# A fused decoder layer: one hidden combination split before it is stored, and an order of work moved

## What is computed

```
x = x + gate2 * (square(relu(h @ w_mlp1)) @ w_mlp2)      # w_mlp1 1024 x 4096, w_mlp2 4096 x 1024
```

## Time and profile before

| what | us |
|---|---|
| median of 3 runs (lowest, highest) | 1138.2 (1137.73, 1141.65) |
| the profiled execution's own time | 1139.7 |
| its span, first to last instruction | 1137.8 |
| PE busy | 1092.3 (96%) |
| DVE busy | 769.6 (68%) |
| ACT busy | 441.9 (39%) |
| POOL busy | 248.7 (22%) |
| TensorE's granted clock, mean share of 2.4 GHz | 0.988 |

### The profile page before, as it was taken

How to read it: one execution, slowest core, us unless ns; L and a number is a source line. 1 busy time by engine, 2 the same in 40 slices (tenths; PEclk the granted TensorE clock), 3 DMA queues, 4 the chain that set the end, 5 groups by cost and what they waited for, 6 DMA issues and landing times. The chain is left out here.

```text
span 1137.8 us, 14053 instructions
## 1 busy us (share of the span) xinstructions
PE 1092.3 (96%) x5210; PEld 882.9 (78%) x5210; DVE 769.6 (68%) x1206; ACT 441.9 (39%) x746; POOL 248.7 (22%) x219
## 2 busy tenths in 40 slices
PE   5999999999999999998999999999899899999998
PEld 4678877777778988776788888887678788787787
DVE  5673556565446767799676767677886957848752
ACT  6342334354444335662333323233522514416231
POOL 2011000000001105213222222223223314232231
PEclk9999999999999999998999999999999999999999
DMA  9967333332013013104535353537626345335205
GB/s 272 275 185 259 128 114 111 112 111 74 28 38 122 29 47 93 38 0 144 180 114 191 113 193 112 194 111 251 229 93 226 145 148 187 100 121 222 74 1 148
DMA packets 150932, 151.71 MB, mean 133 GB/s; under 512 B 14116, under 2 KB 124880, under 8 KB 147280
## 3 DMA queue, kind: packets, MB, share of 16 engines
q1 hardware_dynamic: 142800, 122.45, 33.5%
q0 software_dynamic: 8064, 28.36, 7.6%
HBM read 113.04 MB, written 37.75 MB: 133 GB/s over the span
## 5 line engine op out<-in xcount | busy, mean ns | idle before, releaser
L745 PE MATMUL ps<-cmb_hi,wm_hi 128*128 128x512 f32 x880 | 349.2, 397 | 25.7 <-DVE x1t L2162 9.9
L746 PE MATMUL ps<-cmb_lo,wm_hi 128*128 128x512 f32 x880 | 345.3, 392 | 0.0
L747 PE MATMUL ps<-cmb_hi,wm_lo 128*128 128x512 f32 x880 | 345.1, 392 | 0.0
L745 PEld LDWEIGHTS ps<-cmb_hi,wm_hi 128*128 128x128 f32 x880 | 166.8, 190 | 69.4 <-DVE x1t L2162 12.7
L747 PEld LDWEIGHTS ps<-cmb_hi,wm_lo 128*128 128x128 f32 x880 | 166.8, 190 | 35.3
L746 PEld LDWEIGHTS ps<-cmb_lo,wm_hi 128*128 128x128 f32 x880 | 166.9, 190 | 34.5 <-issue 0.5
L745 PE MATMUL ps<-act_hi,w_hi 128*128 128x512 f32 x400 | 162.2, 405 | 3.0 <-DVE act_lo L1688 3.0
L746 PE MATMUL ps<-act_lo,w_hi 128*128 128x512 f32 x400 | 156.7, 392 | 0.0
L747 PE MATMUL ps<-act_hi,w_lo 128*128 128x512 f32 x400 | 156.7, 392 | 0.0
L1398 ACT ACTIVATE wm_hi<-wm_f 128x512 fp32r<-128x512 f32 x128 | 77.3, 627 | 197.7 <-POOL wm_f L715 151.8
L2162 DVE SCALAR_TENSOR_TENSOR x1t<-ps,ada,x1t 128x512 f32<-128x512 f32 x112 | 83.5, 746 | 81.5 <-PE ps L747 81.5
(11 more groups left out here) (200 smaller groups left out, 1413.8 us busy)
## 6 DMA issues: line engine op xcount, KB each, us to landing
raw<-in_w_mlp_dram SPq DMA_DIRECT2D x128, 256.0 KB, 3.9
cmb_f<-h_spill SPq DMA_DIRECT2D x22, 1024.0 KB, 4.9
wada<-in_w_ada_dram POOLq DMA_DIRECT2D x32, 512.0 KB, 5.0
h_spill<-stage SPq DMA_DIRECT2D x16, 768.0 KB, 6.3
w_raw<-in_w_in_dram SPq DMA_DIRECT2D x18, 512.0 KB, 3.8
ada_rows<-in_w_ada_dram SPq DMA_DIRECT2D x16, 512.0 KB, 7.4
h_spill<-stage SPq DMA_DIRECT2D x32, 256.0 KB, 3.3
h_spill<-stage SPq DMA_DIRECT2D x16, 512.0 KB, 6.7
```

The source lines that it names most:

```text
L745: pe.matmul(bank, wh, hi, start=first, stop=False, skip_group_check=onto)
L746: pe.matmul(bank, wh, lo, start=False, stop=False, skip_group_check=onto)
L747: return pe.matmul(bank, wl, hi, start=False, stop=last, skip_group_check=onto)
```

## The change

T2 is no longer stored whole and split again for each chunk. In the up phase ScalarE rounds T2's slot of stage into a new tile sums_high (`hidden_hi`), VectorE subtracts it in place (`hidden_lo`), and SyncE stores the two as two transfers of 256 KB into a new tensor split_spill (`store_split`); T1 and T3 are stored as 512 KB. For a chunk, T2 is loaded as two transfers of 1 MB straight into cmb_hi and cmb_lo, and product S2 of a chunk's first step waits for both landings (32) in place of low pieces. combination_hi and both_lo of T2 are gone. sums_high takes 2 KB of x1t's last tile, so that tile is stored at the start of the up phase and loaded back at step 18 (512 KB each), and add_product(19, 3) waits for it.

The order is changed: at pair 2 e1(3) and c11(3) come later, SyncE's order at pairs 2, 14 and 15 is another (T1, T3 and T2 of chunk 0 are loaded before pair 14's stores), e2(15) moves from pair 15 to step 16, T1's low pieces stand after S1's weights, T3's first low piece ahead of add_product(w, 0), and step 16's list of VectorE is rearranged; chunk 1's early loads go from step 17 to step 18. Left out of the diff: new semaphores, the size of h_spill (6 in place of 7 combinations) and split_spill, and the renumbering of `piece`.

```diff
--- before
+++ after
@@ -90,9 +90,14 @@
...
     _more = _p + 1 < PAIRS
+    if _p == 2:
+        UP_COPIES += [("e5", 2), ("e1", 3), ("e2", 2)]
+        UP_SUMS += [("e25", 2), ("c22", 2), ("c11", 3), ("c12", 2), ("c21", 2)]
+        SQUARES += [("b21", 1), ("b11", 2), ("b22", 2), ("b11", 3), ("b12", 2)]
+        continue
     UP_COPIES += [("e1", _p + 1)] * _more + [("e5", _p), ("e2", _p)]
     UP_SUMS += [("c11", _p + 1)] * _more + [("e25", _p), ("c22", _p), ("c12", _p), ("c21", _p)]
-    SQUARES += [("b21", _p - 1)] + [("b11", 2)] * (_p == 2) + [("b11", _p + 1)] * _more + [("b22", _p), ("b12", _p)]
+    SQUARES += [("b21", _p - 1)] + [("b11", _p + 1)] * _more + [("b22", _p), ("b12", _p)]
 SQUARES += [("b21", PAIRS - 1)]
@@ -104,8 +109,9 @@
-FIRST_LOADS = (B11, B21, T1, T2, T3, B22, NT4)
-STORED = (B11, B22, T1, T2, T3, B21, NT4)
+STORED = (B11, B22, T1, T3, B21, NT4)
+STORED_SPLIT = (T2,)
+PIECES = (B11, B21, T1, T3, B22, NT4)
@@ -166,6 +172,7 @@
...
         stage = at("stage", [8, HALF], TMPB)
+        sums_high = at("sums_high", [len(STORED_SPLIT), HALF], REG + 28 * KB, F32R)
         early = [at(f"early{i}", [HK, HALF], TMPB + 8 * i * KB) for i in range(2)]
@@ -562,11 +572,20 @@
...
                 sp.wait_ge(s_tt, 4 * p + 3)
-                store(p, s_stt, slice(2, 5), slice(ST_T1, ST_T3 + 1))
+                store(p, s_stt, slice(2, 4), slice(ST_T1, ST_T3 + 1, 2))
...
                 sp.wait_ge(s_tt, 4 * p + 4)
-                store(p, s_stb21, slice(5, 7), slice(ST_B21, ST_NT4 + 1))
+                store(p, s_stb21, slice(len(STORED) - 2, len(STORED)), slice(ST_B21, ST_NT4 + 1))
+            def store_split(p):
+                q, j = divmod(p, CHUNK_PAIRS)
+                sp.wait_ge(s_hth, p + 1)
+                sp.dma_start(split_spill[q, 0, :, :, j, :].rearrange("i p n -> p i n"),
+                             sums_high[:, :, :].bitcast(F32)).then_inc(s_sth, 16)
+                sp.wait_ge(s_htl, p + 1)
+                sp.dma_start(split_spill[q, 1, :, :, j, :].rearrange("i p n -> p i n"),
+                             stage[:, SPLIT_SLOTS, :]).then_inc(s_stl, 16)
@@ -574,17 +593,29 @@
...
                 sp.wait_ge(s_pd, PRODUCT[PAIRS - 1 + CHUNK_PAIRS * q, i])
-                load_combination(q, i, cmb_f[i])
+                if i in STORED_SPLIT:
+                    n = STORED_SPLIT.index(i)
+                    sp.dma_start(cmb_hi[i][:, :, :].bitcast(F32), split_spill[q, 0, n]).then_inc(s_cl[i], 16)
+                    sp.dma_start(cmb_lo[i][:, :, :].bitcast(F32), split_spill[q, 1, n]).then_inc(s_cl[i], 16)
+                else:
+                    load_combination(q, i, cmb_f[i])
             def hidden_stored(q):
-                for s in (s_stb11, s_stb22, s_stt, s_stb21):
+                for s in (s_stb11, s_stb22, s_stt, s_stb21, s_sth, s_stl):
                     sp.wait_ge(s, 16 * CHUNK_PAIRS * (q + 1))
+            sp.wait_ge(s_evb, 2 * N_OUT)
+            sp.dma_start(x_spill[KT - 1], x1t[:, KT - 1, :]).then_inc(s_x1out, 16)
             for p in range(PAIRS):
+                if p == PAIRS - 1:
+                    load_in_place(0, T1)
                 sp.wait_ge(s_wlm, SPLIT[p, A22])
...
                 load_pair(p + 2)
+                if p == PAIRS - 1:
+                    load_in_place(0, T3)
+                    load_in_place(0, T2)
                 if p:
@@ -593,23 +624,33 @@
...
                 if p == 1:
+                    store_split(0)
                     store_b22(1)
...
                     store_b11(2)
+                    store_b22(2)
+                    store_b11(3)
+                    store_split(1)
+                    continue
+                if p + 1 == PAIRS:
+                    store_split(p - 1)
                 if p + 1 < PAIRS:
                     store_b11(p + 1)
+                    store_split(p - 1)
                     if p == PAIRS - 2:
...
                     store_b22(p)
-            for i in FIRST_LOADS[2:]:
+            for i in (B22, NT4):
                 load_in_place(0, i)
...
                 q, pp = divmod(w - PAIRS, CHUNK_PAIRS)
+                if w == PAIRS + 2:
+                    store_split(PAIRS - 1)
                 if w + 2 < 2 * PAIRS:
@@ -617,12 +658,14 @@
...
                     store_b21(PAIRS - 1)
-                if pp == 1 and q + 1 < CHUNKS:
+                if pp == (1 if q else 2) and q + 1 < CHUNKS:
                     hidden_stored(q + 1 if q else CHUNKS - 1)
...
                     load_combination(q + 1, B21, early[1])
+                if w == PAIRS + 2:
+                    sp.dma_start(x1t[:, KT - 1, :], x_spill[KT - 1]).then_inc(s_x1in, 16)
                 if pp == CHUNK_PAIRS - 1 and q + 1 < CHUNKS:
@@ -1149,7 +1192,10 @@
...
                 def wait_part(j):
-                    if j % 2 == 0:
+                    if i in STORED_SPLIT:
+                        if j == 0:
+                            pe.wait_ge(s_cl[i], 32 * (q + 1))
+                    elif j % 2 == 0:
                         pe.wait_ge(s_clo, piece(q, i, j // 2))
@@ -1478,6 +1524,15 @@
...
+            def hidden_hi(p):
+                act.wait_ge(s_tt, 4 * p + 3)
+                if p == 0:
+                    act.wait_ge(s_h2, 2 * KT)
+                    act.wait_ge(s_x1out, 16)
+                wait(act, s_sth, 16 * p)
+                act.activation(sums_high[:, :, :], stage[:, SPLIT_SLOTS, :], ACT.Copy).then_inc(s_hth, 1)
             def combination_hi(q, i):
@@ -1511,24 +1566,28 @@
...
                         e1(2)
-                    if p + 1 < PAIRS:
+                    elif p + 1 < PAIRS:
                         e1(p + 1)
...
                     e5(p)
+                    if p + 1 < PAIRS:
+                        hidden_hi(p - 1)
                 if p and p + 1 < PAIRS:
...
                 weight_hi(p + 1, S1)
+                if p == 2:
+                    e1(3)
                 if p == 0:
                     weight_hi(1, A22)
+                elif p + 1 < PAIRS:
+                    e2(p)
                 else:
-                    e2(p)
+                    hidden_hi(p - 1)
                 if p == PAIRS - 1:
...
                 weight_hi(p + 1, S2)
-                if p == PAIRS - 1:
-                    combination_hi(0, T2)
                 weight_hi(p + 1, S4)
@@ -1552,6 +1611,8 @@
...
                     combination_hi(q, B22)
+                if w == PAIRS:
+                    e2(PAIRS - 1)
                 if ends:
@@ -1564,14 +1625,13 @@
...
                     weight_hi(w + 1, S3)
-                if ends:
-                    combination_hi(q + 1, T2)
-                if more:
                     weight_hi(w + 1, S1)
...
                     weight_hi(w + 1, S2)
+                if w == PAIRS + 1:
+                    hidden_hi(PAIRS - 1)
                 if ends:
@@ -2020,6 +2080,7 @@
...
                 dve.wait_ge(s_sq, n_b12(p))
+                wait(dve, s_stl, 16 * p)
                 dve.tensor_tensor(stage[:, ST_T1, :], b12, b11, ALU.subtract).then_inc(s_tt, 1)
@@ -2030,6 +2091,12 @@
...
                 dve.tensor_tensor(stage[:, ST_NT4, :], stage[:, ST_B21, :], stage[:, ST_T2, :], ALU.subtract).then_inc(s_tt, 1)
+            def hidden_lo(p):
+                dve.wait_ge(s_hth, p + 1)
+                dve.wait_ge(s_tt, 4 * p + 4)
+                dve.tensor_tensor(stage[:, SPLIT_SLOTS, :].bitcast(F32R), stage[:, SPLIT_SLOTS, :], sums_high[:, :, :].bitcast(F32),
+                                  ALU.subtract).then_inc(s_htl, 1)
@@ -2095,6 +2162,7 @@
...
             weight_lo(3, A12)
+            hidden_lo(0)
             squared(ST_B22, n_c22(1))
@@ -2110,14 +2178,13 @@
...
                 last_sum(p - 1)
-                if p == 2:
-                    c11(2)
-                    squared(0, n_c11(2))
                 if p + 1 < PAIRS:
-                    c11(p + 1)
-                    squared((p + 1) % 2, n_c11(p + 1))
+                    b = p + (p > 2)
+                    c11(b)
+                    squared(b % 2, n_c11(b))
                     weight_lo(p + 2, A11)
                     weight_lo(p + 2, A12)
+                    hidden_lo(p - 1)
                 else:
@@ -2125,13 +2192,18 @@
...
                     weight_lo(p + 1, S3)
+                    if p == 2:
+                        c11(3)
+                        squared(1, n_c11(3))
                     c12(p)
...
                     both_lo(0, B21)
-                    both_lo(0, T1)
                     weight_lo(p + 1, S3)
                 weight_lo(p + 1, S1)
+                if p + 1 == PAIRS:
+                    hidden_lo(p - 1)
+                    both_lo(0, T1)
                 weight_lo(p + 1, S2)
@@ -2151,12 +2223,16 @@
...
                 yield
+                hidden_lo(p)
+                yield
...
                 m, e = 2 * ((w - PAIRS) % CHUNK_PAIRS) + o, 7 * (w - PAIRS) + i
+                if (w, i) == (PAIRS + CHUNK_PAIRS - 1, 3):
+                    dve.wait_ge(s_x1in, 16)
```

(34 more changed lines are left out.)

12 lines of the change are left out of this document (8 added, 4 removed).

## The result

| kernel | median, us (lowest, highest) | profiled execution: time, span |
|---|---|---|
| before | 1138.76 (1137.73, 1141.65), 6 runs | 1139.7, 1137.8 |
| after | 1130.99 (1129.01, 1133.45), 6 runs | 1129.01, 1127.2 |

The ratio is 0.9928, 95% interval 0.9916 to 0.9939: 0.7% faster, 7.8 us. The forecast was 14.9 us less, 1123.3, in a range that ended at 1130.0. The direction was right, the size about half, and the result lies outside the range.

A forecast was written before the change was run, and what follows sets the result against it. TensorE, busy 96% of the span, was taken as the bound, with only idle time and clock to win. Terms -3.1 - 4.4 + 0.6 - 8.0 = -14.9 took 1138.2 to 1123.3 us, range 1118.5 to 1130.

The forecast's parts named there:

- Pair 2: Up phase, pair 2: the pauses before products S4 and A22 both go, -3.1 us.
- Pairs 3 to 14: Up phase, forecast for pairs 3 to 13: the split's added copy and subtraction stay hidden, cost 0.
- Steps 17 to 19: Step 17: hidden_lo(15) ahead of add_product(18, 0) lengthens the wait of product S2, 0.76 already, by +0.6 us.
- Borders: Three later chunk borders: one pause of about 1.3 us stays at each, the second goes, -8.0 us together.
- The handover: Pair 15 and step 16, up to down: 10.8 us lost becomes 6.4, -4.4 us.
- The pause of 3.46 goes: Step 16, before product T2: T1 lands earlier, VectorE runs through, and the 3.46 us wait disappears.
- T2's low part is the fifth megabyte from then: Handover load queue: counted from T1's issue at about 786.8 us, T2's low part lands near 803.
- 1.7 for a clock that does not fall: Handover: a stretch of half clock after a pause goes, 1.7 us of the -4.4.
- Its pause grows from 2.20 to 2.7: Pair 15, product A22: B21 lands 0.5 us later, so the wait for c22 grows to 2.7 us.
- NT4's forecast pause of 1.5: Step 16: NT4's pieces and weight A11 ahead of add_product(16, 4) make product NT4 wait 1.5 us.
- the handover gives nothing: Rival: B21 lands 3 to 4 us late, product A22's pause grows as much, +4.4, 1127.7 us; chance 0.11.
- The rival that both falls stay: Rival: the clock falls as often as before, both dips stay, +3.4, 1126.7 us; chance 0.17.

The follow-up runs named there:

- x4: Kernel before with only pair 2's new order (e1(3), c11(3) later, stores reordered), T2 stored whole: 1134.71 us, ratio 0.9966.
- x3: Kernel after with T2's low part loaded behind T1 at the three chunk borders: 1130.23 us, ratio 0.9934.
- the repeats: Kernel after, unchanged, run twice more: 1133.81 us (ratio 0.9947) and 1131.51 us (0.9923).
- x2: Kernel after with chunk 0's loads of B22 and NT4 issued ahead of pair 14's stores: 1133.37 us, ratio 0.9951.
- x6: Kernel after with pair 15's A22 weights rounded on ScalarE ahead of the copies of B11 and B21: 1128.97 us, ratio 0.9908.
- y1: Kernel after with the store of x1t's last tile, and its wait, behind pair 2's raw weight loads: 1130.61 us, ratio 0.9923.
- y2: Kernel after with the moves of x3, x5, x6 and y1, hidden_lo(1) behind pair 2's square, sums between B11's and NT4's low pieces: 1120.06 us, ratio 0.9829.
- x1: Kernel after with B22's first low piece in step 16 moved behind add_product(16, 2): 1132.96 us, ratio 0.9950.
- x5: Kernel after with x2's early loads, e2(15) behind NT4's high copy and A11's weights behind NT4's sum: 1127.61 us, ratio 0.9896.

## Why the prediction came out as it did

**Pair 2: right mechanism, one length off.** x4's stage is 3.1 shorter, as forecast. The forecast counted the new subtraction as one of five slots "of about 0.65 us"; it measured 1.79 beside GpSimd in the profiled run, and product A22 waited 0.62 for c22. That the Trainium skill has VectorE and GpSimd shut each other out (SBUF — State Buffer, Who interferes with whom) was cited for NT4's pieces and not applied here; the row agrees with it.

**Pairs 3 to 14: right**, no pause in any execution.

**Steps 17 to 19: right**, 1.36 against 0.76.

**Borders: right.** T1 was late for the reason given, which x3 shows for about half of the pause; the pause that stayed was 1.26 where 1.3 stood, NT4's went: -7.6 against -8.0. The forecast's own sum had a slip: a pause of 1.3 with its 0.29 is 1.6 and not 1.4, which makes the three borders -7.4.

**The handover: the failed step.** "The pause of 3.46 goes": it did. The step that failed is the load queue, the sentences "T2's low part is the fifth megabyte from then: 4.8 + 4 x 2.4 + some 2 for the raw weights among them, near 803" and, built on it, "B22 and NT4 ... land near 810 and 812", with T3's pause put at 0.65. The forecast has T2's low part 16.4 us behind T1's issue and B22 23.2 us behind it (786.8 to 810). In the kernel after, T1 left at 783.15, T2's low part landed 18.9 us later (issued at 789.35, 12.7 us to landing) and B22 25.9 us later. The last 7 us, from T2's low part to B22, are as forecast; the stretch up to it was priced 2.5 us too short, although the forecast counted it high: T1, the raw weights, T3 and T2's two parts are five megabytes with the raw weights in, which at 4.8 + 4 x 2.4 would be 14.4. T3 waited 3.15 for it. That stretch, with the columns of the earlier trace rows:

```profile
783.00:786.00 3.00, 3.00 (x15) 2.49 (x14) 0.58 (x1) 2.38 (x3) 1.38 (x2) 1.00 0.56 182
786.00:807.00 21.00, 17.54 (x77) 13.84 (x76) 20.08 (x23) 8.37 (x12) 4.70 (x3) 1.00 0.98 355
```

For the first 3 us the queue held T1 alone, since the raw weights behind it wait for A22's rounding and left at 786.13. From then on the DMA engines were busy all the time, but moved 355 GB/s and not the 437 of the borders' loads. Which of the two weighs more was not tested. In the repeats the raw weights left 4.6 us behind T1, and B22 landed 27.6 and 28.0 us behind it. That B22's time of day, 809.1, came out as forecast is luck: the whole handover stood 3.6 us earlier than in the rows of before (product S1 of pair 15 began at 780.15 and not at 783.77), and T1's issue with it. x2 shows the queue's part from the other side: with 1.5 MB of stores behind B22 and not ahead of it, it landed 21.4 us behind T1's issue.

Then the clock. "1.7 for a clock that does not fall" became a fall of 6.8 us, 3.4 lost, in all three executions of the kernel after.

"Its pause grows from 2.20 to 2.7": A22's was 2.27, but S4's, which I kept at 0.38, grew to 1.18, and to 2.81 in the repeats. e5(15) waits for the combinations of pair 14, which stand on VectorE behind A22's low weights and so behind ScalarE's rounding of them, which stood behind B21's copies. B21 was there 2.7 us after product S1 of pair 15 began, 3.8 and 4.2 in the repeats, against 1.9 before. x6 shows that order to be the cause: with the rounding ahead of the copies both pauses are gone. NT4's forecast pause of 1.5 did not come, probably since T3's wait gave its pieces time: once that wait was gone (x2) it was 2.97.

Added up for the profiled execution, against the forecast: S4 +0.8, A22 -0.4, T3 +2.5, NT4 -1.8 with its 0.29, clock +3.4, together 4.5, where the stage was 4.2 longer than forecast. Lost in the handover, over 35.4: 10.6 before, 10.4, 11.7 and 12.4 after; the forecast had 10.8 and 6.4.

The rival "the handover gives nothing" had a chance of 0.11 and the time 1127.7. Its outcome is what happened, but not by its mechanism: B21 came 0.8 to 2.3 us later against TensorE and not 3 to 4, and the larger part came by B22 and the clock.

**Pairs 0 and 1: not in the sum at all.** The forecast spoke of x1t's store nowhere, though the diff puts a wait on SyncE ahead of load_pair(2). It makes the first stage 1.4 to 1.7 us longer (y1 takes that back). Pair 1 was 1.1 shorter in the same executions, by 3.4 us less of half clock, and 0.3 to 0.6 us of loss is left of the two. That the shorter half clock comes from the later raw weights is not shown: pair 1 took 22.6 to 22.8 us before, in x4 and in y1, which don't have them, and 21.1 to 21.6 in all that do, but 21.5 in y2, which doesn't either. All that an in-order queue holds behind an added wait must be counted, also 300 us away from where the change aims.

**The clock.** The rival that both falls stay was right in kind: the falls changed place and hardly got fewer. From the first product to the last there were 17.1 us of half clock before and 17.1, 17.1 and 13.7 after; in the handover 3.4 before and 6.8 to 10.2 after. The first border's pause of 2.38 had no fall before, and x4, with the same pause (2.39) at the same border, had one: length alone doesn't decide. The Trainium skill (TensorE: Matmul & The Clock Gate, What's actually happening) says that the gate looks at windows that run free of the kernel, which fits; yet T3's pause had a fall in it in all six executions that had the pause, while x1's 3.06 before NT4 had none and y2's 1.88 before T2 had one.

## What to carry to other kernels

Count a landing from the first issue of its queue, against the product that the issue waits for, and not as a time of day of the old trace; ask what stands still behind that issue; and price a queue of loads, weights and stores at the rate of a row with the same mixture. Here the rate of loads alone was 2.5 us too short over five megabytes. A wait behind a late landing moves from product to product: the early loads showed no gain in the time (x2) until ScalarE's and VectorE's order let them through (x5). And put a pair of long low pieces on either side of the sum that TensorE waits for, not ahead of it.
